# Paged attention scores: pages at two partition offsets, and five sample slots per recurrent block in place of four

## What is computed

```python
def mla_sample(q_nope, q_pe, ckv, kpe, pool_ckv, pool_kpe, layer_idx, page_table, w_ukv):
    ...
    q_lat = jnp.einsum('bshn,chn->bshc', q_nope, w_uk)
    ckv_past = pool_ckv[layer_idx, page_table].reshape(db, -1, A_KV_LORA)
    kpe_past = pool_kpe[layer_idx, page_table].reshape(db, -1, A_ROPE)
    ...
    sc_past = (jnp.einsum('bshc,btc->bhst', q_lat, ckv_past)
               + jnp.einsum('bshr,btr->bhst', q_pe, kpe_past)).astype(jnp.float32) * SM_SCALE
    ...
    p = jax.nn.softmax(jnp.concatenate([sc_past, sc_self], axis=-1), axis=-1).astype(ckv.dtype)
    o_lat = (jnp.einsum('bhst,btc->bshc', p[..., :n_past], ckv_past)
             + jnp.einsum('bhst,btc->bshc', p[..., n_past:], ckv))
```

## Time and profile before

| | us |
|---|---|
| median of 3 runs | 2274.91 (2271.66 to 2275.79) |
| the profiled execution | 2284.63 |
| its span | 2282.9 |
| PE busy over the span | 2185.3 (96%) |
| DVE busy | 1036.6 (45%) |
| ACT busy | 730.8 (32%) |
| recurrence, states, keys and values, prompt heads | 128, 46, 37, 120.5 |

### The profile page before, as it was taken

One profiled execution on the slowest core, in us unless ns is written; L12 is line 12 of the kernel. 1 busy time (PEld: TensorE's weight loads), 2 busy tenths in 40 slices (PEclk: granted clock), 3 DMA queues, 4 the chain that ended last, 5 costly groups with the idle time before them and its releaser, 6 DMA issues.

```text
span 2282.9 us, 46816 instructions
## 1 busy us (share of the span) xinstructions
PE 2185.3 (96%) x18285; PEld 2072.4 (91%) x18285; DVE 1036.6 (45%) x2002; ACT 730.8 (32%) x1292; POOL 120.2 (5%) x226
## 2 busy tenths in 40 slices
PE   8999999998776789999999999999999999999997
PEld 8999999997443458999999999999999999999997
DVE  5444434366654344544433444443446664444333
ACT  6222223354212333422222232222232233222222
POOL 0000000001234241000000000000000000000000
PEclk9999999998887789999999999999999999999999
DMA  4222223234799872222222222222322222222222
GB/s 162 92 92 92 92 102 100 81 125 147 213 265 279 236 212 93 84 92 92 92 92 100 97 91 91 92 92 92 102 92 92 92 93 92 88 87 91 94 100 75
DMA packets 101037, 261.98 MB, mean 115 GB/s; under 512 B 14385, under 2 KB 49218, under 8 KB 100866
## 3 DMA queue, kind: packets, MB, share of 16 engines
q1 hardware_dynamic: 89746, 228.83, 31.6%
q0 software_dynamic: 11184, 31.69, 4.7%
HBM read 255.29 MB, written 5.16 MB: 114 GB/s over the span
## 4 chain that ended last, share of the span: by engine, by line
PE 61%; DVE 1%; ACT 0%; issue 0%; DVEq 0%; ACTq 0%
PE bank L279 20%; PE bank L278 20%; PE bank L280 20%; PE bank L1929 1%; PE bank L1908 0%; PE bank L303 0%; DVE sb_x L1012 0%; PE bank L1921 0%; PE bank L1700 0%; PE bank L1943 0%; DVE sb_x L373 0%; ACT L312 0%; ACT sb_t L343 0%; DVE sb_h_lo L351 0%; ACT sb_h_hi L338 0%
## 5 line engine op out<-in xcount | busy, mean ns | idle before, releaser
L278 PE MATMUL bank<-sb_h_hi,sb_w_hi 128*128 128x260 f32 x3552 | 1005.9, 283 | 9.8 <-DVE sb_h_lo L1471 8.2
L279 PE MATMUL bank<-sb_h_lo,sb_w_hi 128*128 128x260 f32 x3552 | 1007.1, 284 | 0.0
L280 PE MATMUL bank<-sb_h_hi,sb_w_lo 128*128 128x260 f32 x3552 | 1003.8, 283 | 0.0
L250 ACT ACTIVATE sb_w_hi<-sb_raw 128x1024 fp32r<-128x1024 f32 x339 | 359.7, 1061 | 1260.8 <-PE bank L280 1257.1
L278 PEld LDWEIGHTS bank<-sb_h_hi,sb_w_hi 128*128 128x128 f32 x3552 | 668.5, 188 | 11.5 <-DVE sb_w_lo L256 8.3
L280 PEld LDWEIGHTS bank<-sb_h_hi,sb_w_lo 128*128 128x128 f32 x3552 | 671.4, 189 | 0.0
L279 PEld LDWEIGHTS bank<-sb_h_lo,sb_w_hi 128*128 128x128 f32 x3552 | 668.1, 188 | 0.2
L256 DVE TENSOR_TENSOR sb_w_lo<-sb_raw,sb_w_hi 128x1024 fp32r<-128x1024 f32 x339 | 415.3, 1225 | 382.4 <-ACT sb_w_hi L250 381.6
L279 PE MATMUL bank<-sb_a_lo,sb_w_hi 128*128 128x260 f32 x1408 | 399.1, 283 | 0.0
L278 PE MATMUL bank<-sb_a_hi,sb_w_hi 128*128 128x260 f32 x1408 | 398.7, 283 | 0.0
L280 PE MATMUL bank<-sb_a_hi,sb_w_lo 128*128 128x260 f32 x1408 | 397.7, 282 | 0.0
(11 more groups left out here) (279 smaller groups left out, 1556.3 us busy)
## 6 DMA issues: line engine op xcount, KB each, us to landing
sb_raw<-in_w SPq DMA_DIRECT2D x339, 512.0 KB, 3.5
sb_s_raw<-in_cache SPq DMA_DIRECT2D x256, 144.0 KB, 4.7
sb_v_raw<-in_cache POOLq DMA_DIRECT2D x192, 128.0 KB, 5.3
sb_v_raw<-in_cache SPq DMA_DIRECT2D x64, 128.0 KB, 5.8
sb_x<-in_x SPq DMA_DIRECT2D x4, 520.0 KB, 6.2
out_y<-sb_x SPq DMA_DIRECT2D x8, 260.0 KB, 2.3
sb_st<-in_state POOLq DMA_DIRECT2D x8, 256.0 KB, 8.2
out_state_s<-sb_st POOLq DMA_DIRECT2D x8, 256.0 KB, 5.7
```

Source lines behind the costliest of these rows:

```text
L250: nc.scalar.activation(w_hi[slot][:], raw[slot][:], ACT.Copy).then_inc(S("w_hi_done"), 1)
L278: nc.tensor.matmul(out, wh, xh, start=first and c == 0, stop=False)
L279: nc.tensor.matmul(out, wh, xl, start=False, stop=False)
L280: mm = nc.tensor.matmul(out, wl, xh, start=False, stop=last and c == chunks - 1)
```

## The change

Two things are changed together.

**Two places for score pages.** The pages of even quads go to partitions 0 to 95 as before, those of odd quads to partitions 32 to 127 (`LOW` = 32). Each is still one transfer of 144 KB. For that the row of `cache` in DRAM holds the first 32 of the 96 score rows a second time behind them, and an odd page is read from 32 rows further on: its partitions 32 to 95 hold rows 32 to 95, and its partitions 96 to 127 hold rows 0 to 31. The row of `cache` grows from 278,528 to 327,680 bytes. On the query side rows 96 to 127 of `sb_q_s` get a copy of rows 0 to 31 by one more DVE copy (`q_s_ready` counts one step more). The matmuls of an odd quad contract all 128 partitions; partitions 0 to 31 of the four odd slots are zeroed once, by four POOL memsets behind `state_in(1)`, and PE waits for them (`s_cleared`) before quad 1.

**Five slots per recurrent block.** `after_hgrn` lets out five slots in a block (one before the outer products, one between them and the block's output, three after it); every later `after_` function is shifted by 16. So the stages of the sample states and of the keys and values keep 16 slots and 12 slots as before, with the work of one sample later, and the prompt heads keep 47 slots over their 140 steps in place of 63.

```diff
         def after_hgrn(m, part):
-            return 4 * m + part + 1
+            return 5 * m + part + 1 + (part > 1)
...
         def after_prompt(t):
 
-            return min(SLOTS, 96 + (t + 1) * (SLOTS - 96) // PROMPT_SLOTS_IN)
+            return min(SLOTS, 112 + (t + 1) * (SLOTS - 112) // PROMPT_SLOTS_IN)
...
         HB = HEADS * BATCH_D
-        Q_S_STEPS = SK + 2
+        Q_S_STEPS = SK + 3
+        LOW = P - SR
...
-            rows, lo, width = (SR, 0, S_W) if kind == "s" else (PAGE, SR * S_W, KV_LORA)
+            low = LOW if k // COLG % 2 else 0
+            to, rows, lo, width = (low, SR, low * S_W, S_W) if kind == "s" else (0, PAGE, P * S_W, KV_LORA)
             for j in range(JOB):
-                eng.dma_start(slots[k % RING][0:rows, j, :],
+                eng.dma_start(slots[k % RING][to:to + rows, j, :],
...
             state_in(0)
             state_in(1)
+            pool.wait_ge(S("half_done"), 2 * U0["ukv"])
+            for i in range(COLG, RING):
+                pool.memset(s_raw[i][0:LOW], 0.0).then_inc(S("s_cleared"), 1)
             pool.wait_ge(S("q_lat_mm"), 1)
...
+                dve.wait_ge(S("q_s_ready"), Q_S_STEPS - 1)
+                dve.tensor_copy(q_s[SR:P, :, :, 0:HEADS], q_s[0:LOW, :, :, 0:HEADS]).then_inc(S("q_s_ready"), 1)
...
                 quad_loaded(pe, "s", n)
+                rows = slice(0, SR if n % 2 == 0 else P)
+                if n == 1:
+                    pe.wait_ge(S("s_cleared"), COLG)
                 for c in range(SK):
                     for j in range(COLG):
...
-                        last = mm(out, q_s[0:SR, i, c, :], s_raw[(COLG * n + j) % RING][0:SR, :, c * P:(c + 1) * P],
+                        last = mm(out, q_s[rows, i, c, :], s_raw[(COLG * n + j) % RING][rows, :, c * P:(c + 1) * P],
...
-    cache = np.concatenate([both.reshape(POOL, -1), lat.reshape(POOL, -1)], axis=1)
+    cache = np.concatenate([both.reshape(POOL, -1), both[:, :P - SR].reshape(POOL, -1), lat.reshape(POOL, -1)], axis=1)
```

More of the change, by code:

```diff
@@ L413, in after_hgrn @@
         def after_hgrn(m, part):
-            return 4 * m + part + 1
+            return 5 * m + part + 1 + (part > 1)
         def after_state(u):
-            return 65 + u + 1
+            return 81 + u + 1
         def after_norm(n):
-            return 73 + n + 1
+            return 89 + n + 1
         def after_kv(s):
-            return 84 + s
+            return 100 + s
         def after_prompt(t):
-            return min(SLOTS, 96 + (t + 1) * (SLOTS - 96) // PROMPT_SLOTS_IN)
+            return min(SLOTS, 112 + (t + 1) * (SLOTS - 112) // PROMPT_SLOTS_IN)
         def prompt_at(t):
```

## The result

The changed kernel is slower: 2297.99 us median (2295.13 to 2302.42, 4 runs) against 2274.37, ratio 1.0088, 95% interval 1.007 to 1.0106, that is +16 to +24 us. Forecast were 2281 (2260 to 2297). The profiled execution took 2296.57 us, its span is 2294.9.

The account below looks back on a forecast made before the run. The prediction took page transfers to bound the recurrence and PE with its small waits the prompt heads. Terms 26 - 4 - 17 + 0.3 + 1.0 gave +6.3 us, 2290.9 profiled and 2281 as the median, range 2260 to 2297.

Parts of the forecast that it names:

- the difference is carried over unchanged: Final sum: the profiled execution's 9.7 us above the median was assumed to stay, turning 2290.9 into 2281.
- +26: Recurrence: five slots per block at the old transfer rate lengthen the stage by 22 to 31 us, taken as +26.
- 1.3 for the small terms: Recurrence: 0.3 us for the longer DVE copy plus 1.0 for state steps delayed by quads ahead of outer products.
- quad 5 is slot 23 ... one block earlier, between 587 and 593 us: Recurrence: five slots bring quad 5 forward from 599.24 us, leaving 57 slots that take 120 to 123 us.
- a block that goes no faster than its pages come: Late recurrence blocks: page transfers set the pace, 8.62 us per quad, so DVE's 19.2 us wait lies inside.
- the load is evened only where pages of an even and of an odd quad are in flight together: Score-page transfers: reason for expecting little from two places, since mostly one place is in flight; range 0 to +15%.
- +2.5% of rate: Page transfers: gain from two places, giving back 3 us in the recurrence and 1 in later stages, -4 together.
- Taking the mix apart: Late recurrence transfers: values at 403 GB/s leave scores 202, so the partitions a transfer covers set its rate.
- -17 forecast: Prompt heads: nine tenths of 19.0 us, from 14.0 of PE work and 5.0 of idle time; range 12 to 20.
- late pages on the chain (2295): Recurrence rival: quads ahead of outer products wait for pages, delaying DVE's state steps; about +20 us, chance 0.15.
- the rate rises (2267 and 2275): Transfer rivals: balanced halves reach about 300 GB/s, 2267, chance 0.25; or the rate gains 6%, 2275, chance 0.04.
- pages are not what holds the stage (2271): Recurrence rival: the slots go into PE's idle time, growth at most 12.5 us, sum -4; chance 0.06.

Follow-up runs that it names:

- e5: Changed kernel with DVE's sample steps moved behind the next block's state steps (slots 0 and 1: behind the masks); ratio 1.0044 to the kernel before.
- e6: Changed kernel loading only the left half of each page's columns after the first two quads; ratio 0.9994 to the kernel before.
- e11: Five slots, DVE's sample steps behind the next block's state steps, and half of each page loaded after two quads; ratio 0.9890 to the kernel before.
- e7: Kernel before, loading only the left half of each page's columns after the first two quads; ratio 0.9920 to the kernel before.
- e10: Kernel before with only DVE's sample steps moved behind the next block's state steps; ratio 0.9970 to the kernel before.
- e1: Changed kernel with four slots per block as before, so only the two places by quad; ratio 0.9998 to the kernel before.
- e3: Four slots per block, score pages alternating between the two places from job to job inside a quad; ratio 0.9975 to the kernel before.
- e2: Kernel before with five slots per block, all score pages in one place; ratio 1.0095 to the kernel before.

## Why the prediction came out as it did

The sign held, the centre did not: +6.3 was forecast, +16 to +24 came. The median lies 1 us above the range's upper end, the ratio times the earlier median (1.0088 x 2274.91 = 2295) 2 us below it. Between the two profiled executions it is +12: the terms of the sum are 6 us off, and they would be further off if the recurrence (10 us too small) and the heads (7 us too small a gain) didn't err in opposite directions, which is luck. The rest is the step "the difference is carried over unchanged": the profile of before lay 9.7 us above its median, that of the changed kernel 1.4 below.

**The recurrence: mis-sized, +24 forecast (+26, less 3 for the rate, 1.3 for the small terms), +34 measured.** The step that failed is "quad 5 is slot 23 ... one block earlier, between 587 and 593 us". PE's score quads in the changed kernel, the fifth quad (number 4) and number 5:

```profile
590.82 1.50 PE L1695 MATMUL bank<-sb_s_raw,sb_q_s 96*32 96x256 f32 x24 [0.97 <-ACT sb_s_all L762]
...
599.14 1.48 PE L1695 MATMUL bank<-sb_s_raw,sb_q_s 128*32 128x256 f32 x24
```

Quad 5 starts at 599.14, before at 599.24: a block earlier in the count, not in time, since the blocks had become longer. The other half of the step was right: the 57 slots from there took 719.0 - 599.1 = 119.9 us, forecast 120 to 123. With the new order (e5) quad 5 comes at 592.4 and the stage takes 155.1, +27 over before, near the +26 that was worked out for pages at the old rate:

```profile
592.45 1.48 PE L1693 MATMUL bank<-sb_s_raw,sb_q_s 128*32 128x256 f32 x24
```

What was left out is the order on DVE: the diff moved its sample steps as well as PE's, and the prediction looked at the quads' place on PE alone. It shows where the order costs time. Up to quad 5 the changed kernel takes 42.1 us and e5 35.4; from there on 119.9 and 119.7, so with whole pages a block like the one shown above would have been held by its pages for about as long. With half pages the later stretch shows the order too: 112.0 us in e6, 99.3 in e11.

**What bounds the stage: half right.** That a late block is "a block that goes no faster than its pages come" is not the whole of it. In the kernel before, half the bytes shorten the recurrence by 9.5 us (e7) and the new order alone by 8.1 (e10), so both limits lay close together. In the changed kernel half the bytes give 10.3 us (e6), the order 6.9 (e5), both together 28.3 (e11). Neither alone shows more than a part, because the other takes over.

**Two places: the reason against was right, the size too high.** The prediction said that "the load is evened only where pages of an even and of an odd quad are in flight together", and so it was: by quad nothing came (e1), by job 0.25% (e3). The +2.5% of rate and the -4 us were not there. The Trainium skill's page "SBUF — State Buffer", section "Can I just issue two DMAs to hit both halves?", has two concurrent DMAs, one on each half, at only +6% over one. The traces agree with a gain that small, on other partitions (0 to 95 and 32 to 127): 265 GB/s in e3 against 259 in e1. Taking the mix apart into 202 GB/s for scores and laying that on the halves was argued from rows, and e3 speaks against it: with both places in flight the mix stays far below 403. What holds it there is open.

**The small costs: right.** POOL's timeline and DVE's copy in the changed kernel:

```profile
559.23 2.79 POOL L578 MEMSET sb_s_raw<- 32x768 f32 x4
561.95 3.17 POOL L468 DMA_DIRECT2D sb_v_raw<-in_cache  x6
```

```profile
L1170 DVE COPY sb_q_s<-sb_q_s 32x192 f32<-32x192 f32 x1 | 0.3, 253 | 0.0
```

2.9 us of memsets were forecast and nobody waits for them; the copy takes 0.25, forecast 0.3. A score quad of 128 rows takes 1.48 us where one of 96 takes 1.50 (the rows of quads 5 and 4 above).

**The heads: mis-sized the other way, -17 forecast, -24 measured** (-22.5 between e1 and e2). Score quads in the heads of the changed kernel, to set beside the earlier trace rows:

```profile
L1710 PE MATMUL bank<-sb_v_raw,sb_p_t 128*32 128x256 f32 x160 | 11.6, 408 | 0.0
L1695 PE MATMUL bank<-sb_s_raw,sb_q_s 128*32 128x256 f32 (+1 forms) x120 | 9.4, 448 | 3.8 <-ACT sb_s_all L762 3.8
```

PE work fell by 16.3 us in the window (101.09 to 84.78), more than the 12.6 that nine tenths of 14.0 are, and idle time by 7.8 where 4.5 were counted. All 3.9 us of waits for score pages went, not four ninths of them; they were a single wait, so a share by count was the wrong measure.

**The rivals.** The one that came nearest in time, late pages on the chain (2295), had the place right and the cause wrong. The outer products' wait did grow beyond 19.2 us, to 34.0, but waits for score pages fell from 2.9 to 1.1 (for value pages they rose from 1.2 to 2.4): DVE was late because it waited for PE's sample work, not because pages were. That the rate rises (2267 and 2275) is ruled out by e1 and by the changed kernel's own 256 GB/s. That pages are not what holds the stage (2271) is ruled out by the +34 us, where it gave 12.5 at most; e6 shows what was right in it, that pages are not the only limit.

## What to carry to other kernels

When work is threaded between the steps of a loop on several engines, moving it is a change of every engine's order; go through each engine that the loop's chain passes, and ask what its next chain step now stands behind. A period that divides evenly (16 slots over four blocks) can hide part of such a wait, and another one brings it out. Before a queue of transfers is called the only limit, halve the bytes and keep everything else: here that took only 10 of 162 us off a stage with a DMA share of 0.99 over most of it. And where two limits lie close together, remove both: one alone shows only the part that the other doesn't take over.

## What was not expected of the hardware

A stage can show its DMA engines full and still not be held by them alone: the changed kernel's recurrence runs at share 0.89 and 238 GB/s, at 0.99 and 256 from 600 us on, and at 0.49 and 137 GB/s (e6) it is only 6% shorter. Alternating the two places from job to job (two transfers each) moved the mix of score and value pages from 259 to 265 GB/s over 600 to 685 us, where value pages and state stores without score pages move 403.
